# A two-layer trunk step on one core: half of the output weights loaded a stage earlier, the first tile's output product moved ahead of the other tiles', three of four score blocks kept in SBUF

## The reference, cut to what matters

```python
x = x + gate1 * (o @ w_out)                         # o: 640 x 1024, w_out: 1024 x 1024
h = rms_norm(x, g) * (1 + scale2) + shift2
q  = (h @ peer_wq).reshape(tokens, 8, 2, 128)       # peer_wq: 1024 x 2048
s1 = q[:, :, 0] . k1                                # 128 scores per head, twice
s2 = q[:, :, 1] . k2
v1, i1 = top_k(s1, 16);  v2, i2 = top_k(s2, 16)     # then the 16 best of the 256 sums
idx = expert numbers (16 per head, 128 per token, out of 16384)
act = gelu(U[idx] . h)                              # U, V: 16384 rows of 1024 per layer
x = x + gate2 * sum_k softmax_k * act_k * V[idx_k]
```

## Time and profile before

| | |
|---|---|
| median of 3 runs | 5055.29 us (5054.23 to 5055.33) |
| the profiled execution, its own time | 5056.95 us |
| its span, first to last instruction | 5055.2 us |
| busy: PE / DVE / POOL / ACT | 62% / 78% / 55% / 14% of the span |
| moved by DMA | 1504 MB, of it 1342 MB gathers |
| stage_experts, layer 1 | from 839.6 us to about 2648 us |
| stage_experts, layer 2 | from 3264.0 us to 5055 us |

### The profile page before, as it was taken

The page is one execution under the profiler, slowest core; times in us unless marked ns, Lnnn a source line. Parts: engine busy times, 40 slices in busy tenths (PEclk is TensorE's granted clock), DMA queues, the critical chain, the costliest instruction groups (busy, mean ns, idle before and its releaser), DMA issues. The chain is left out here.

```text
span 5055.2 us, 39175 instructions
## 1 busy us (share of the span) xinstructions
PE 3152.6 (62%) x11894; PEld 1710.1 (34%) x11894; DVE 3952.1 (78%) x7486; ACT 726.3 (14%) x1734; POOL 2773.2 (55%) x2867
## 2 busy tenths in 40 slices
PE   8989869887136063077977995988722705407227
PEld 3368736542012021023425882754201201102012
DVE  6847675898897997988754767579979799799875
ACT  2112222211001010012111222321100101001001
POOL 0023240667777766776661324056777777677776
PEclk9989959999679587598998995999966958859669
DMA  8600002799999999999992000169999999999999
GB/s 305 222 18 1 8 28 76 295 413 408 410 402 409 410 397 410 399 407 391 416 381 113 2 1 25 75 238 412 410 409 403 409 407 399 410 410 398 410 398 366
DMA packets 438055, 1504.23 MB, mean 298 GB/s; under 512 B 47308, under 2 KB 55620, under 8 KB 436054
## 3 DMA queue, kind: packets, MB, share of 16 engines
q0 software_dynamic: 368640, 1342.34, 66.9%
q1 hardware_dynamic: 69208, 159.39, 8.8%
HBM read 1487.21 MB, written 11.73 MB: 297 GB/s over the span
## 5 line engine op out<-in xcount | busy, mean ns | idle before, releaser
L2002 PE MATMUL ps<-z,o 128*128 128x512 f32 x2356 | 1165.2, 621 | 526.1 <-DMA z<-in_peer_v,experts 333.9
L2038 DVE CUSTOM_DVE_ANT_0 z<-z,ps 128x1024 f32<-128x1024 f32 x1176 | 1417.8, 1218 | 80.1 <-DMA z<-in_peer_u,experts 39.7
L1725 POOL DMA_INDIRECT z<-in_peer_u,experts x1176 | 1110.5, 944 | 501.6 <-issue 209.9
L1725 POOL DMA_INDIRECT z<-in_peer_v,experts x1178 | 1120.8, 951 | 461.3 <-issue 275.1
L2063 DVE SCALAR_TENSOR_TENSOR ps<-z,state,ps 128x1024 f32<-128x1024 f32 x579 | 743.6, 1284 | 338.8 <-DMA z<-in_peer_v,experts 338.6
L2002 PEld LDWEIGHTS ps<-z,o 128*128 128x128 f32 x2356 | 413.3, 194 | 1272.5 <-ACT o L1841 751.4
L1856 PE MATMUL ps<-const,hT 128*128 128x128 f32 x80 | 17.8, 397 | 1043.2 <-ACT o L1841 1043.2
L1841 ACT ACTIVATE o<-const,state 128x128 f32<-128x128 f32 x640 | 244.7, 399 | 1076.4 <-PE ps L2002 1071.8
L1856 PEld LDWEIGHTS ps<-const,hT 128*128 128x128 f32 x80 | 14.4, 207 | 1048.5 <-ACT o L1841 1016.2
L1868 PE MATMUL ps<-hT,w 128*128 128x512 f32 x512 | 223.7, 593 | 0.0
L844 POOL TENSOR_TENSOR kn<-kn,neg_half 128x4 f32<-128x4 f32 x20 | 20.1, 1008 | 342.3 <-DVE kn L887 313.8
(11 more groups left out here) (424 smaller groups left out, 5243.5 us busy)
## 6 DMA issues: line engine op xcount, KB each, us to landing
gate<-in_w_mod SPq DMA_DIRECT2D x80, 512.0 KB, 4.7
w<-in_w_in SPq DMA_DIRECT2D x15, 2048.0 KB, 11.3
z<-in_peer_v,experts POOLq DMA_INDIRECT x1178, 12.2
z<-in_peer_u,experts POOLq DMA_INDIRECT x1176, 13.8
w<-in_peer_wq SPq DMA_DIRECT2D x8, 2048.0 KB, 19.4
w<-in_w_out SPq DMA_DIRECT2D x4, 2048.0 KB, 11.2
z<-in_peer_wq SPq DMA_DIRECT2D x4, 2048.0 KB, 18.1
scores<-rows SPq DMA_DIRECT2D x8, 1024.0 KB, 17.1
```

The source lines that it names most:

```text
L1725: eng.indirect_dma_start(slot, None, at_layer_rows(table), bass.IndirectOffsetOnAxis(ap=m.experts[:, t % 2, k:k + 1], axis=0)).then_inc(lo ...
L2002: mm = eng.matmul(m.ps[:, 4 + n, :], m.diag[:, (done + q) % DIAGS, :], row_j[:, n * 512:(n + 1) * 512], start=(q == 0), stop=(q == SLOTS / ...
L2038: eng.tensor_tensor_reduce(row_j, row_j, h_rows, 1.0, 0.0, ALU.mult, ALU.add, m.acts[:, k:k + 1]).then_inc(used_v, 1)
```

## The change

- In `stage_attention`, SP loads the first half of `w_out` behind the gates and waits for it at the stage's end. The buffers change place for it: `we[0]` lies in the region `rows` (whose parameters are no longer read then), and what lay there (keys, `score_out`, `out_tmp`, `xs`, four of the late ring's slots) goes to the region of `w[0]`. In `stage_experts` only the second half is left to load.
- Tile 0 of `o` is transposed alone, in two halves of four chunks, copied by one ACT and one DVE instruction of 128 x 512. Products 0 and 1 follow. The other tiles' chunks are turned behind them (`turn_rest`): five before `turn_x(0)`, two behind it, one inside `first(0)`. Product 2 moves behind `first(1)`.
- On DVE the gating of product 2 comes behind the first pair's ranking, and one more product (3) between the dots. On POOL its addition comes before gather 2. The tables are set anew.
- Only the scores of block 3 are stored to HBM (one store of 1 MB a layer) and loaded by tile (four loads of 256 KB). Those of blocks 0, 1 and 2 stay in SBUF and are read by the ranking in place.
- In layer 1, SP waits for the last tile's ranking before it loads the first `w_in` blocks.

```diff
@@ stage_attention, SP
+                w_out = at_layer(m.inp["w_out"], l).rearrange("(c p) n -> p c n", p=P)
+                eng.dma_start(m.we[0], w_out[:, :, 0:512]).then_inc(w_out_loaded, 16)
                 eng.wait_ge(gates_loaded, 64)
+                eng.wait_ge(w_out_loaded, 16)
@@ rank_step
-            elif h == 0:
+            elif h // 2 == STORED_BLOCK:
                 eng.wait_ge(sems.scores_loaded, 16 * t)
...
+            src = m.score_tile[:, a, :] if t == 0 or h // 2 == STORED_BLOCK else m.score_kept[h // 2][:, t - 1, c, :]
@@ stage_experts
-    ADD_BEFORE = {2: 3, 7: 4, 12: 5, 18: 6, 22: 7, 26: 8, 30: 9}
-    RSTD_BEFORE = {4: 1, 14: 2, 24: 3, 31: 4}
+    ADD_BEFORE = {2: 2, 7: 3, 12: 4, 17: 5, 22: 6, 26: 7, 28: 8, 30: 9}
+    RSTD_BEFORE = {9: 1, 19: 2, 27: 3, 31: 4}
@@ stage_experts, SP
-                    eng.wait_ge(*rest_s_kept("list", PER * (p + 1) - 1))
-                    eng.dma_start(m.scores[:, :, PER * n:PER * (n + 1), :].rearrange("t p j n -> p t j n"),
-                                  m.score_out).then_inc(scores_stored, 16)
-                eng.wait_ge(scores_stored, 16 * NB)
+                    if n == STORED_BLOCK:
+                        eng.wait_ge(*rest_s_kept("list", PER * (p + 1) - 1))
+                        eng.dma_start(m.scores.rearrange("t p j n -> p t j n"), m.score_out).then_inc(scores_stored, 16)
+                eng.wait_ge(scores_stored, 16)
                 for t in range(1, TILES):
                     eng.wait_ge(sems.keys_ranked, t)
-                    eng.dma_start(m.score_tile, m.scores[t - 1]).then_inc(sems.scores_loaded, 16)
+                    eng.dma_start(m.score_tile[:, PER * STORED_BLOCK:PER * (STORED_BLOCK + 1), :], m.scores[t - 1]).then_inc(sems.scores_loaded, 16)
...
+                        if n == 0:
+                            eng.wait_ge(sems.keys_ranked, TILES)
@@ stage_experts, ACT, keep_rest_s
-                    if j >= PER and j % PER == 0:
-                        eng.wait_ge(scores_stored, 16 * (j // PER))
+                    if j == 0:
+                        eng.wait_ge(*out_gated("block", OUTS - 1))
+                    if j == 2 * PER:
+                        eng.wait_ge(scores_stored, 16)
@@ stage_experts, PE
+                def turn_rest(c):
+                    if c >= 2:
+                        eng.wait_ge(*o_kept("chunk", c - 2))
                     for t in range(1, TILES):
+                        mm = eng.transpose(m.ps[:, c % 2, (t - 1) * P:t * P], m.o[:, t, c * P:(c + 1) * P], ident)
                     mm.then_inc(o_turned.sem, o_turned.one("chunk", c))
...
-                for i in range(3):
-                    output(i)
+                output(0)
+                output(1)
+                for c in range(5):
+                    turn_rest(c)
                 turn_x(0)
+                turn_rest(5)
+                turn_rest(6)
                 first(0)
                 first(1)
+                eng.wait_ge(*o_kept("chunk", KC - 1))
                 turn_h(0)
-                for i in range(3, 6):
+                for i in range(2, 6):
                     output(i)
@@ stage_experts, DVE
-                GATE_BEHIND = {1: 4, 6: 5, 12: 6, 16: 7, 18: 8, 20: 9}
+                GATE_BEHIND = {1: 3, 6: 4, 11: 5, 17: 6, 20: 7, 22: 8, 24: 9}
```

More of the change, by code:

```diff
@@ L1639, in _ @@
                 src = at_layer(m.inp["peer_wq"], l).rearrange("(c p) n -> p c n", p=P)
-                for n in range(2):
-                    eng.dma_start(m.w[n], w_out[:, :, n * 512:(n + 1) * 512]).then_inc(w_out_loaded[n], 16)
+                eng.dma_start(m.we[1], w_out[:, :, 512:1024]).then_inc(w_out_loaded, 16)
                 eng.dma_start(m.wq_first[0], src[:, :, 0:512]).then_inc(wq_first_loaded[0], 16)
@@ L1692, in _ @@
                 rstd(0)
-                add_output(2)
                 for t in range(TILES):
@@ L1737, in square @@
                         eng.wait_ge(*tile_turned("tile", t - 2))
-                    eng.activation(m.xs[t % 2], m.x[:, t, :], ACT.Square, scale=float(D) ** -0.5,
+                    eng.activation(m.xs[(t + 1) % 2], m.x[:, t, :], ACT.Square, scale=float(D) ** -0.5,
                                    accum_out=m.small[:, t:t + 1]).then_inc(squares.sem, squares.one("tile", t))
@@ L1743, in scale_rest @@
                     eng.wait_ge(*squares("tile", t))
-                    eng.activation(m.xs[t % 2], m.x[:, t, :], ACT.Copy, scale=m.small[:, 16 + t:17 + t]).then_inc(
+                    eng.activation(m.xs[(t + 1) % 2], m.x[:, t, :], ACT.Copy, scale=m.small[:, 16 + t:17 + t]).then_inc(
                         rest_scaled.sem, rest_scaled.one("tile", t - 1))
@@ L1770, in keep_rest_s @@
                     eng.wait_ge(*rest_s("list", j))
[L1771 to L1773 removed]
+                    n = WQ_ORDER[j // PER]
+                    if j == 0:
+                        eng.wait_ge(*out_gated("block", OUTS - 1))
+                    if j == 2 * PER:
+                        eng.wait_ge(scores_stored, 16)
+                    at = m.score_out if n == STORED_BLOCK else m.score_kept[n]
+                    eng.activation(at[:, :, j % PER, :], m.ps[:, 4 + j % 2, :].rearrange("p (t n) -> p t n", t=TILES - 1),
                                    ACT.Copy).then_inc(rest_s_kept.sem, rest_s_kept.one("list", j))
[L1776 to L1778 removed]
+                eng.wait_ge(*o_first_turned("half", 0))
+                eng.activation(m.hT[:, 0:4, 0:P], m.ps[:, 2, :].rearrange("p (c n) -> p c n", c=4), ACT.Copy).then_inc(o_first_kept_a, 1)
                 square(0)
@@ L1887, in output @@
                     t, n = i // 2, i % 2
-                    if t == 0:
-                        eng.wait_ge(w_out_loaded[n], 16)
+                    if t == 0 and n == 1:
+                        eng.wait_ge(w_out_loaded, 16)
                     if i >= 2:
@@ L2018, in gate_output, with keep_rest_o @@
                                       ALU.mult).then_inc(out_gated.sem, out_gated.one("block", i))
-                for c in range(KC):
+                def keep_rest_o(c):
                     eng.wait_ge(*o_turned("chunk", c))
-                    eng.tensor_copy(m.hT[:, c, P:TOK], m.ps[:, 2 * (c % 2), :]).then_inc(o_kept_v.sem, o_kept_v.one("chunk", c))
-                for i in range(3):
+                    eng.tensor_copy(m.hT[:, c, P:TOK], m.ps[:, c % 2, :]).then_inc(o_kept.sem, o_kept.one("chunk", c))
+                eng.wait_ge(*o_first_turned("half", 1))
+                eng.tensor_copy(m.hT[:, 4:8, 0:P], m.ps[:, 3, :].rearrange("p (c n) -> p c n", c=4)).then_inc(o_first_kept_v, 1)
+                for i in range(2):
                     gate_output(i)
+                for c in range(5):
+                    keep_rest_o(c)
                 eng.wait_ge(*rstd_ready("tile", 0))
-                eng.tensor_scalar(m.xs[0], m.x[:, 0, :], m.small[:, 16:17], None, ALU.mult).then_inc(first_scaled, 1)
+                eng.tensor_scalar(m.xs[1], m.x[:, 0, :], m.small[:, 16:17], None, ALU.mult).then_inc(first_scaled, 1)
                 eng.wait_ge(*tile_turned("tile", 0))
@@ L2031, in _ @@
                 ins.then_inc(h_first, 1)
+                for c in range(5, KC):
+                    keep_rest_o(c)
                 def dot(t, k):
@@ L2237, in place @@
     m.acts, m.cube, m.weight, m.share = m.state[0][:, 0, :], m.state[0][:, 1, :], m.state[1][:, 0, :], m.state[1][:, 1, :]
-    m.late_ring = ([m.rows[:, s * D:(s + 1) * D] for s in range(4)] + [m.gate[:, 0, s, :] for s in range(2)]
+    m.late_ring = ([wall[:, s * D:(s + 1) * D] for s in range(4)] + [m.gate[:, 0, s, :] for s in range(2)]
                    + [m.const[:, P + s * D:P + (s + 1) * D] for s in range(2)]
@@ L2298, in declare @@
     m.gates = nc.dram_tensor("gates", (DEPTH, 2, 2, D), F32, kind="Internal").ap()
-    m.scores = nc.dram_tensor("scores", (TILES - 1, P, 2 * HEADS, NKEY), F32, kind="Internal").ap()
+    m.scores = nc.dram_tensor("scores", (TILES - 1, P, 4, NKEY), F32, kind="Internal").ap()
     for name, shape in OUT:
```

60 lines of the change are left out of this document (30 added, 30 removed).

## The result

The changed kernel took 5004.58 us (median of 4 runs, 5002.19 to 5008.89), the kernel before 5055.22 us in the same session: a ratio of 0.9899, 95% interval 0.9883 to 0.9915, so 50.6 us less. I had forecast 5012 us, with a range of 5003 to 5030. The profiled execution took 5002.94 us, 54.0 us less than the profiled one of before.

A forecast was written before the change was run, and what follows sets the result against it. The prediction took the DMA engines, full at some 410 GB/s, as the bound. Start 21.2, gating and block 2 wait -4.4, bytes 30.7, DVE as bound -4: 43.5 us off 5056.95, as a median 5012, range 5003 to 5030.

The forecast's parts named there:

- The bytes: Score stores and loads in the full stream: 6.29 MB less a layer at 410 GB/s, 15.3 us a layer, 30.7 in all.
- The start: Head of the expert stage: first gather earlier by 8.5 us in layer 2 and 12.7 in layer 1, 21.2 in all.
- Up to 0.7 lost: Head, DVE: five chunk copies behind product 1 take up to 5.0 us against 4.3 until the root; 0.3 taken.
- The two turns behind the turn of the normed tile lie beside DVE's scale and shift: Head, PE ahead of the first queries: these turns run alongside DVE's work; no gain or loss counted.
- The new wait: DVE at block 2's ranking waits 0 to 3 us for scores, in both layers; 1.5 us a layer taken.
- DVE as the bound in tile 0's row-product phase: DVE bounds tile 0's row-product phase for a while, ring full, DMA idle about 2 us a layer; 4 in all.
- Rival 1: PE takes the head's gain through the wait for block 2's scores; start worth 7 us, 5025 us; chance 0.12.
- Rival 4: TensorE stays at 1.2 GHz from the stage's start to the end of the first scores; slower, 5093 us; chance 0.03.
- rival 6: More gain: the ring covers both losses (8.4 us) behind the first gathers; 5003 us; chance 0.04.
- 2: Rival: bytes saved in the gather stream fill holes only; 5038 us; chance 0.05.
- 3: Rival: small score loads cost as much as large, 17 us given back; 5029 us; chance 0.07.
- 5, no change: Rival: DVE or POOL bound the stream, so both gains are waited away; 5055 us; chance 0.03.

The follow-up runs named there:

- e3: Changed kernel plus some 6.5 us of repeated DVE work ahead of tile 0's first pair's ranking, delaying the first gather; 5018.59 us.
- e1: Changed kernel with the old DMA bytes put back: all four score blocks stored, each tile loads 1 MB, ranking unchanged; 5034.92 us.
- e10: Changed kernel with order and early `w_out` load of the head undone, only the kept scores left; 5027.43 us, kernel before 5058.03 us.
- e12: Changed kernel with tile 0's first pair ranked head by head, first 16 gathers waiting for head 0 alone, POOL's additions shifted; 4999.10 us.
- e9: The changed kernel unaltered, rerun as reference on another chip; 5008.34 us, kernel before 5058.03 us.
- e4: Changed kernel plus some 6.5 us of repeated DVE work ahead of the third pair's ranking (block 2), behind the first 32 gathers; 5015.14 us.
- e2: Changed kernel where each tile loads its 256 KB score block four times, 24 more loads in all; 5022.15 us.
- e8: Changed kernel with turns of chunks 5 and 6 moved inside `first(0)`, behind its products; 5507.41 us on a chip where the kernel before took 5539.47.
- e5: The changed kernel unaltered, on a chip with a thinner stream; 5503.06 us, kernel before 5539.47 us.

## Why the prediction was right

**The bound.** It held that the stage ends when the DMA engines have moved all bytes, and that only an earlier first gather and fewer bytes count. e3 (12.3 to 14.0 us for 13) and e1 and e10 (28.6 to 30.3, and 30.6 us for 30.7) show both at nearly their full price; e10 to e12 have the start at 0.73 to 0.87 of it.

**The bytes.** 30.7 forecast, 28.6 to 30.6 measured. The small loads cost 0.66 to 0.73 us each where I took 0.64: over eight of them at most 0.7 us.

**The start.** 21.2 forecast, 10.0 + 13.5 = 23.5 in the trace. The step "the first product starts 2.4 us into the stage" was 0.5 us too careful (1.94). "Up to 0.7 lost" to the five copies ahead of the scaling was nothing: they end as the root is ready. "The two turns behind the turn of the normed tile lie beside DVE's scale and shift" missed their effect on the clock: `first(0)` ran at 1.00 and took 7.4 us, not 9.05. That was 1.6 us a layer that I had not counted. In layer 2 the way from the scaling to `first(0)` became 0.8 us longer (5.44 us, before 4.63), since the clock fell over the turns themselves; in layer 1 it did not (4.64). As e9 and e12 show, part of this gain is luck: with the clock's fall a little elsewhere `first(0)` takes 9.0 us with the turns too.

**The new wait.** 1.5 us a layer forecast, 1.16 measured in layer 2 and none in layer 1, where I had expected the same as in layer 2. The load of `peer_wq` ahead of it landed in 14.4 us, as the guess "or earlier" allowed. That time lost at this place is mostly paid is shown by e4.

**The term that failed** is "DVE as the bound in tile 0's row-product phase: the ring runs full and DMA idles for about 2 us a layer", 4 us in all. DVE did become busy without a break, but DMA did not idle. Stretches of layer 2 after:

```profile
3420.00:3440.00 20.00, 20.00 (x59) 9.85 (x59) 20.00 (x48) 2.58 (x5) 11.77 (x11) 1.00 1.03 409
3440.00:3460.00 20.00, 20.00 (x71) 10.86 (x70) 20.00 (x37) 3.96 (x7) 14.72 (x16) 1.00 1.03 414
3460.00:3480.00 20.00, 20.00 (x54) 9.40 (x53) 18.28 (x32) 1.80 (x4) 15.12 (x17) 1.00 1.03 409
3480.00:3500.00 20.00, 11.51 (x48) 7.04 (x47) 18.52 (x38) 5.18 (x13) 13.40 (x15) 0.81 1.03 410
```

DVE is busy for 20.00 of 20 us up to 3460 and then again has room (18.28, 18.52), while the DMA share stays at 1.03. The phase ended 15.9 us earlier, where my sum allowed DVE 12.7, since it started 10.0 and not 8.5 us earlier and lost less on the way. With that term at zero and the start as measured the sum is 23.5 - 4.4 + 30.7 = 49.8 us, against 50.6 measured by the medians. With the new wait as measured too it is 51.6. That the sum comes out within 1 us is in part chance: single prices scatter by 2 us between sessions, and the profiled executions differ by 54.0.

So the mechanism was right, and every miss lay on one side: the gain came out 7 us larger than forecast, since the start was 2.3 us too careful, the new wait 1.8 and the loss to DVE 4. These make 8.1 us, of which 7.1 reached the medians.

Three sums of the prediction don't come out as written. Rival 1's is 5055.3 - 7 - 30.7 = 5017.6, or 5021.6 with the 4 us that stand there, and not 5025; it lies closer to the forecast than I said. Rival 4's two stretches hold 52.5 us of work at the full clock, which at the low level would take 50 us more, not 55. And losses of 0 to 16 us make 5003 to 5019, so that the forecast's own stretch should have begun at 5003: the measured time lies in it then, and rival 6 was no rival but its lower end.

**The rivals.** 1 falls by e3, 2 by e1 and e10, 3 by e2. 4, TensorE at 1.2 GHz, falls by the rows of after (a granted clock of 0.95 over the head). Its mechanism is real all the same: e8 shows the clock low behind a wait of 2.74 us, and the new order mostly escapes this because it put turns into the wait. That is also where the Trainium skill's rule on waits between matmuls ("TensorE: Matmul & The Clock Gate", section Loop structure matters more than you think) and the trace agree. 5, no change, falls by the result. 6, with all losses covered (5003), came nearest: of the 8.4 us of loss 0.8 are left by the two profiled executions (54.1 by start and bytes, 53.3 at the stages' ends) and 3.6 by the medians.

**What did not fit** is `w_in` in layer 1, whose loads I named as a risk: two of them moved from tile 2's row-sum phase into tile 3's (1877.4 us before, 2184.1 after), and the end of the stage hardly waited for them, if at all (27.4 us earlier, 28.8 by start and bytes). The 3 us by which tile 0's row-sum phase in layer 2 is ahead of start and bytes (10.0 + 3.93 MB at 410 GB/s = 19.6, measured 22.7), given back by the end of the stage, stay unexplained.

## What to carry to other kernels

Find the stretch in which one resource is full, and price an edit by two numbers: how much earlier the stretch starts (here 0.7 to all of it reached the end), and how much less goes through it at its measured rate; the time from a transfer's issue to its landing is no price there. Where a chain of engines hands over to one another ahead of it, look at what can be cut out of the first piece and ranked or copied for a part only, and put short work that has to be done anyway into TensorE's waits; here it spared the matmuls behind them the low clock in most stages, not in all. Test each part of an edit in the presence of the others, and make sure first that the stream on the chip at hand is full: where it had holes, the same edit was worth 7 us in place of 30.

## What the runs showed of the hardware that was not expected

Eight more turns in a wait of 2.7 us changed the granted clock over the 64 matmuls behind it from 0.71 to 1.00, and their time from 10.25 to 7.41 us (e8 and e5). In two of eighteen stages with these turns (layer 1 of e9 and e12) the clock fell over the turns and stayed low into the matmuls, which took 9.0 us.

A load in a full stream lands in about the same time whether it is 256 KB (8.6 us) or 1024 KB (8.0 us), and takes from the stream hardly more than its bytes (0.66 to 0.73 us where the bytes take 0.64, and by e1 28.6 to 30.3 us for 12.58 MB).

The same kernels took 5539 us before and 5503 us after on one of the chips, with most slices at 350 to 390 GB/s and stretches of 20 us and more without any gather. In the one that was followed, ACT had stood still for 16 and 21 us with its inputs ready; why it did stays open.
